# Three attention projection units moved in among the forms and first steps of the recurrence's first pair; query and key rotation released four copies sooner

## What is computed

```python
h = rms_norm(x, ln1_g[l]) * (1.0 + scale1) + shift1
z = jnp.einsum('bsd,de->bse', h, w_in[l])
y_a = rwkv7_time_mix(z_rwkv, ...)
y_b = moba_attention(z_att, q_norm_g[l], k_norm_g[l])
merged = g_a * (y_a @ w_br_rwkv) + g_b * (y_b @ w_br_moba)
x = x + gate1 * (merged @ w_out)
x = x + gate2 * hierarchical_moe(h2, ...)
```

## Time and profile before

| what | us |
|---|---|
| median of 3 runs | 1046.7 (1045.08 to 1047.42) |
| the profiled execution's own time | 1044.92 |
| its span in the trace | 1043.0 |
| PE busy in the span | 996.4 (96%) |
| DVE, ACT, POOL busy | 526.4, 319.5, 130.0 |

### The profile page before, as it was taken

How to read it: one execution, slowest core, us unless ns; L and a number is a source line. 1 busy time by engine, 2 the same in 40 slices (tenths; PEclk the granted TensorE clock), 3 DMA queues, 4 the chain that set the end, 5 groups by cost and what they waited for, 6 DMA issues and landing times.

```text
span 1043.0 us, 17857 instructions
## 1 busy us (share of the span) xinstructions
PE 996.4 (96%) x7746; PEld 633.3 (61%) x7746; DVE 526.4 (50%) x809; ACT 319.5 (31%) x587; POOL 130.0 (12%) x152
## 2 busy tenths in 40 slices
PE   8999999998888899999999999999999999999998
PEld 6777899978775588788787333444344434344343
DVE  4668852146538875676566433433344333342354
ACT  4467743154546731232423211111111111111110
POOL 0000000376974400000001000000000000000000
PEclk9999999999989999999999999999999999999999
DMA  9622021000003078464779999999999999999993
GB/s 384 246 115 98 24 82 44 11 5 4 4 21 145 8 238 298 131 212 176 283 305 397 333 417 428 426 426 427 427 427 425 427 426 426 426 427 419 414 415 133
DMA packets 42975, 273.24 MB, mean 262 GB/s; under 512 B 8032, under 2 KB 8176, under 8 KB 28688
## 3 DMA queue, kind: packets, MB, share of 16 engines
q1 hardware_dynamic: 39488, 264.42, 63.0%
q0 software_dynamic: 2400, 4.28, 1.2%
q10 hardware_dynamic: 1008, 3.38, 0.9%
HBM read 272.06 MB, written 4.19 MB: 265 GB/s over the span
## 4 chain that ended last, share of the span: by engine, by line
PE 80%; DMA 8%; DVE 7%; ACT 3%; issue 1%; SPq 0%; DVEq 0%; POOLq 0%; ACTq 0%
PE banks L1777 30%; PE banks L2336 19%; PE banks L2350 9%; DMA w_tok<-in_w 4%; DMA w_qkv<-in_w 3%; PE banks L2374 2%; PE banks L2375 2%; PE banks L2342 2%; PE banks L2322 1%; ACT xT L977 1%; PE banks L1940 1%; PE banks L1955 1%; PE banks L1957 1%; DVE ring L1397 1%; PE banks L1915 1%
## 5 line engine op out<-in xcount | busy, mean ns | idle before, releaser
L1656 DVE TENSOR_TENSOR hid<-banks,silu_a 64x512 f32<-64x512 f32 x32 | 22.2, 693 | 199.1 <-ACT silu_a L982 199.1
L2350 PE MATMUL banks<-w_ring,hidT 128*64 128x512 f32 x512 | 116.8, 598 | 1.1 <-ACT hidT L986 1.1
L1643 DVE SCALAR_TENSOR_TENSOR mod<-banks,row_weight,mod 64x512 f32<-64x512 f32 x64 | 47.9, 748 | 70.3 <-PE banks L2350 69.3
L982 ACT ACTIVATE silu_a<-banks 64x512 f32<-64x512 f32 x32 | 18.9, 591 | 207.7 <-PE banks L2337 207.7
L2337 PE MATMUL banks<-w_tok,xT 128*64 128x512 f32 x176 | 79.6, 606 | 0.0
L2336 PE MATMUL banks<-w_tok,xT 128*64 128x512 f32 x176 | 78.3, 596 | 0.3 <-DMA w_ring<-in_w 0.3
L2337 PE MATMUL banks<-w_ring,xT 128*64 128x512 f32 x176 | 78.3, 596 | 0.0
L1650 DVE TENSOR_TENSOR x<-x,banks 128x1024 f32<-128x1024 f32 x60 | 71.8, 1219 | 12.6 <-PE banks L2375 12.2
L2336 PE MATMUL banks<-w_ring,xT 128*64 128x512 f32 x160 | 72.4, 606 | 3.3 <-DMA w_qkv<-in_w 3.3
L2350 PEld LDWEIGHTS banks<-w_ring,hidT 128*64 128x64 f32 x512 | 34.3, 136 | 67.0 <-issue 65.8
L1777 PE MATMUL banks<-x_r,ring_r 128*128 128x512 f32 x192 | 74.8, 390 | 0.0
(11 more groups left out here) (387 smaller groups left out, 2180.0 us busy)
## 6 DMA issues: line engine op xcount, KB each, us to landing
w_ring<-in_w SPq DMA_DIRECT2D x42, 2048.0 KB, 25.2
w_tok<-in_w SPq DMA_DIRECT2D x16, 2048.0 KB, 26.0
ada_buf<-in_w_ada SPq DMA_DIRECT2D x64, 256.0 KB, 3.5
w_ab<-in_w SPq DMA_DIRECT2D x8, 2048.0 KB, 25.5
w_qkv<-in_w SPq DMA_DIRECT2D x7, 2048.0 KB, 29.3
w_tok<-in_w SPq DMA_DIRECT2D x24, 512.0 KB, 16.6
w_ring<-in_w SPq DMA_DIRECT2D x24, 512.0 KB, 17.3
w_ring<-in_w SPq DMA_DIRECT2D x10, 1024.0 KB, 15.5
```

What stands on the lines that cost most here:

```text
L1643: dve.scalar_tensor_tensor(dst[:, 512 * n:512 * n + 512], bank[5][SLOTS * n:SLOTS * n + SLOTS, :], weight_of(e), gate2[:, n, :], ALU.mult, ...
L1656: dve.tensor_tensor(hid[:, :], bank[3][SLOTS:P, :], silu_a[:, :], ALU.mult).then_inc(hid_v, 1)
L2350: mm = pe.matmul(bank[5][SLOTS * n:SLOTS * n + SLOTS, :], hidT[:, k, :], w2[:, k, 512 * n:512 * n + 512], start=(k == 0), stop=(k == 3))
```

## The change

Nothing is computed differently; instructions are moved on four engines, and the dummy matmuls of the recurrence are gone.

- PE: forms of groups 0 and 1 come behind unit 20, units 21, 22 and 23 stand between the first steps of pair_a, and the forms of groups 2 and 3 stand between its levels, behind waits on att_out of 11 and 12. Pair_b starts one level of pair_a later than before, so it is two levels behind. Its last steps (m5, wu, gh) run on into the next half. In half 1 the chains and outputs of half 0's last two chunks are spread over more of pair_a's steps.
- ACT and DVE: the same copies and masks in the order that this asks for; ACT takes copy 10 and copy 11 between the recurrence's copies, and the square root (and DVE's reciprocal) for the rotation comes right behind pair_b's r0 and first inverse.
- DVE at the end of half 1: both queries_added of pair_b stand ahead of next_state.
- POOL: the wait on att_out asks for 8 in place of 12.

The diff, cut in ACT's loop, whose rest mirrors the PE loop:

```diff
--- before.py
+++ after.py
@@ -744,8 +744,8 @@
             att_copy(7)
             cut_first("att", 5, 0)
             cut_first("att", 5, 1)
-            for g in range(8, 12):
-                att_copy(g)
+            att_copy(8)
+            att_copy(9)
 
             def end_keys(half, k):
                 sc, g = 2 * half + k // 2, k % 2
@@ -782,43 +782,53 @@
             for k in range(NG):
                 end_keys(0, k)
             act.activation(small[:, 57:58], one, ACT.Sqrt)
+            att_copy(10)
             for half in range(2):
                 solve_copy(half, "x", *pair_a)
                 if half:
+                    solve_copy(0, "h", *pair_b)
+                solve_copy(half, "r0", *pair_a)
+                if half == 0:
+                    att_copy(11)
+                solve_copy(half, "n1", *pair_a)
+                if half:
                     out_copy(0, 2)
-                solve_copy(half, "r0", *pair_a)
+                solve_copy(half, "r1", *pair_a)
                 if half:
                     out_copy(0, 3)
                     for k in pair_b:
                         end_keys(1, k)
-                solve_copy(half, "n1", *pair_a)
-                solve_copy(half, "r1", *pair_a)
+                solve_copy(half, "n2", *pair_a)
+                solve_copy(half, "r2", *pair_a)
                 solve_copy(half, "x", *pair_b)
                 solve_copy(half, "r0", *pair_b)
-                for n in range(2, 5):
+                if half == 0:
+                    act.wait_ge(ssq_qk, 1)
+                    act.activation(rms_qk, ssq, ACT.Sqrt).then_inc(sqrt_qk, 1)
+                for n in range(3, 5):
...
@@ -1015,7 +1025,7 @@
-            pool.wait_ge(att_out, 12)
+            pool.wait_ge(att_out, 8)
@@ -1277,7 +1287,6 @@
-            dve.wait_ge(att_mm, 12)
@@ -1342,37 +1351,47 @@
             for half in range(2):
                 first_inverse(half, *pair_a)
                 if half:
+                    state_factors(0, *pair_b)
+                    queries_added(0, 2)
+                level_masked(half, 1, *pair_a)
+                if half:
                     queries_added(0, 3)
                     next_state(0, 2)
+                else:
+                    masked_forms(0, 2)
+                level_masked(half, 2, *pair_a)
+                if half:
                     next_state(0, 3)
-                level_masked(half, 1, *pair_a)
-                for k in pair_b:
-                    masked_forms(half, k)
-                level_masked(half, 2, *pair_a)
+                    masked_forms(1, 2)
+                masked_forms(half, 3)
+                level_masked(half, 3, *pair_a)
                 first_inverse(half, *pair_b)
-                for n in range(1, 4):
-                    level_masked(half, n, *pair_b)
-                    level_masked(half, n + 2, *pair_a)
-                    if n < 3:
-                        chunk_decays(2 * half + n - 1)
-                level_masked(half, 4, *pair_b)
-                state_factors(half, *pair_a)
-                queries_added(half, 1 - half)
-                level_masked(half, 5, *pair_b)
-                queries_added(half, half)
                 if half == 0:
                     dve.wait_ge(sqrt_qk, 1)
                     dve.reciprocal(ssq, rms_qk).then_inc(rstd_qk, 1)
+                    dve.wait_ge(att_mm, 12)
+                for n in range(1, 3):
+                    level_masked(half, n, *pair_b)
+                    level_masked(half, n + 3, *pair_a)
+                    chunk_decays(2 * half + n - 1)
+                level_masked(half, 3, *pair_b)
+                state_factors(half, *pair_a)
+                level_masked(half, 4, *pair_b)
+                queries_added(half, 1 - half)
+                queries_added(half, half)
+                if half == 0:
                     next_state(0, 1)
+                    level_masked(0, 5, *pair_b)
                     masked_forms(1, 0)
                     masked_forms(1, 1)
                 else:
                     next_state(1, 0)
+                    level_masked(1, 5, *pair_b)
                     next_state(1, 1)
-                state_factors(half, *pair_b)
-                queries_added(half, 2)
+            state_factors(1, *pair_b)
+            queries_added(1, 2)
+            queries_added(1, 3)
             next_state(1, 2)
-            queries_added(1, 3)
 
             def norm_inverse(half):
                 c = slice(256 * half, 256 * half + 256)
@@ -1888,12 +1907,11 @@
-            for u in range(16, 6 * TT):
+            for u in range(16, 21):
                 att_unit(u)
 
-            pe.wait_ge(att_out, 12)
             pe.wait_ge(prep_done, CT)
-            pe.wait_ge(turn_a, TT * CT)
+
             def head_of(k, i):
 
                 h = 4 * (k % 2) + i
@@ -2012,66 +2030,76 @@
                 for _ in range(n):
                     pe.matmul(dst, ident, ident, start=True, stop=True)
 
-            for k in range(NG):
-                forms(0, k)
-                if k < NG - 1:
-                    between(bank[7][:, 0:P], 4)
+            forms(0, 0)
+            forms(0, 1)
+            att_unit(21)
             for half in range(2):
-                for k in pair_a:
-                    if half == 0:
-                        pe.wait_ge(solve_v[k], v_at(0, "tt"))
-                        between(bank[2 * k][:, 256:256 + P], 6)
-                    solve_step(half, "t0", k)
+                solve_step(half, "t0", 0)
+                if half == 0:
+                    att_unit(22)
+                    pe.wait_ge(turn_a, TT * CT)
+                solve_step(half, "t0", 1)
+                solve_step(half, "x", *pair_a)
+                if half:
+                    solve_step(0, "gh", *pair_b)
+                solve_step(half, "r0", *pair_a)
+                if half == 0:
+                    att_unit(23)
+                solve_step(half, "p1", *pair_a)
                 if half:
                     chain(0, 2)
-                solve_step(half, "x", *pair_a)
+                else:
+                    pe.wait_ge(att_out, 11)
+                    forms(0, 2)
+                solve_step(half, "n1", *pair_a)
                 if half:
                     outputs(0, 2)
-                solve_step(half, "r0", *pair_a)
+                else:
+                    pe.wait_ge(att_out, 12)
+                    forms(0, 3)
+                solve_step(half, "r1", *pair_a)
                 if half:
                     chain(0, 3)
-                solve_step(half, "p1", *pair_a)
+                solve_step(half, "p2", *pair_a)
                 if half:
                     outputs(0, 3)
                     forms(1, 2)
                     forms(1, 3)
-                solve_step(half, "n1", *pair_a)
-                solve_step(half, "r1", *pair_a)
+                solve_step(half, "n2", *pair_a)
+                solve_step(half, "r2", *pair_a)
                 solve_step(half, "t0", *pair_b)
-                solve_step(half, "p2", *pair_a)
+                solve_step(half, "p3", *pair_a)
                 solve_step(half, "x", *pair_b)
                 solve_step(half, "r0", *pair_b)
-                for n in range(2, 5):
+                for n in range(3, 5):
                     solve_step(half, f"n{n}", *pair_a)
-                    solve_step(half, f"p{n - 1}", *pair_b)
+                    solve_step(half, f"p{n - 2}", *pair_b)
                     solve_step(half, f"r{n}", *pair_a)
-                    solve_step(half, f"n{n - 1}", *pair_b)
+                    solve_step(half, f"n{n - 2}", *pair_b)
                     solve_step(half, f"p{n + 1}", *pair_a)
-                    solve_step(half, f"r{n - 1}", *pair_b)
+                    solve_step(half, f"r{n - 2}", *pair_b)
                 solve_step(half, "m5", *pair_a)
+                solve_step(half, "p3", *pair_b)
+                solve_step(half, "wu", *pair_a)
+                solve_step(half, "n3", *pair_b)
+                solve_step(half, "gh", *pair_a)
+                solve_step(half, "r3", *pair_b)
                 solve_step(half, "p4", *pair_b)
-                solve_step(half, "wu", *pair_a)
+                if half:
+                    chain(1, 0)
                 solve_step(half, "n4", *pair_b)
-                solve_step(half, "gh", *pair_a)
+                outputs(half, 0)
                 solve_step(half, "r4", *pair_b)
+                chain(half, 1)
+                outputs(half, 1)
                 solve_step(half, "p5", *pair_b)
                 if half == 0:
-                    outputs(0, 0)
-                    solve_step(0, "m5", *pair_b)
-                    chain(0, 1)
-                    outputs(0, 1)
                     forms(1, 0)
-                    solve_step(0, "wu", *pair_b)
+                solve_step(half, "m5", *pair_b)
+                if half == 0:
                     forms(1, 1)
-                    solve_step(0, "gh", *pair_b)
-                else:
```

(9 more changed lines are left out.)

16 lines of the change are left out of this document (8 added, 8 removed).

## The result

The changed kernel takes 1039.65 us (median of 5 runs, 1036.47 to 1040.1) against 1046.7 (5 runs, 1044.07 to 1048.81): a ratio of 0.9926 with a 95% interval of 0.9901 to 0.9951, 7.1 us less. The forecast was 8.8 less, 1037.9. Its profiled execution took 1040.1 us, with a span of 1038.3.

What follows compares the result with a forecast made beforehand. The recurrence was taken as bound by a ring of short dependent steps through PE's in-order queue: its work plus gaps. Gains 7.3 − 0.5 + 2.0 = 8.8 us took the 1046.7 median to 1037.9, range 1034.0 to 1042.2.

Steps and rivals of the forecast that it cites:

- Stretch one: Recurrence up to r0 of pair_b in half 0 (219.88 before): r0 at 212.6, a gain of 7.3 us.
- The second way of counting: Stretch to pair_b's r0, half 0: dummies 6.3, copy 11 wait 0.7, t0 waits 1.5, others 0.5, level costs 1.7; claimed 7.3.
- Stretch two: From there to r0 of pair_b in half 1 (268.15 before): net cost 0.5 us, between 0 and 2.
- Stretch three: From r0 of pair_b in half 1 to the recurrence's end: net gain 2.0 us, between 0.5 and 3.5.
- the clock term: PE's falls to 1.2 GHz in the recurrence: same cost as before, 2.8 us less or more as ends.
- tail: End of half 1, queries ahead of next_state: PE's 1.4 us wait and part of the chain's go, 1.9 us gained.
- The rotation: POOL starts 23.6 us earlier, rotation from near 215 to 269, ACT without a wait; its earlier end costed at nothing.
- Downstream one to one: Merge and experts: a recurrence that ends earlier moves their start, and the expert loads' start, by as much.
- Rival 1: Two-level lag's PE gaps lower the clock twice more, stretch two at upper bound: gain 4.5, 1042.2 us; chance 0.09.
- Rival 2: Norms come late, ACT waits with the recurrence's copies queued behind: 7.9 us slower, 1054.6 us; chance 0.04.
- Rival 3: Merge or experts wait for something the earlier stage does not move: 1046.7 ± 1 us; chance 0.03.
- Rival 4: Units among the forms delay pair_a, stretch one gives only the dummies: gain 6.1, 1040.6 us; chance 0.09.

Runs made afterwards that it cites:

- the changed kernel's second: The changed kernel itself, unedited, timed and profiled again beside other kernels on one chip: 1039.25 us (8 runs), ratio 0.993.
- the units alone: Kernel before with units 21 to 23 among the forms, no dummies, POOL's wait at 8, pair_b one level behind, old tail and square root: 1037.94 us.
- the two cures: Changed kernel with, ahead of chain(1, 0) in half 1, either six dummy matmuls (1031.61 us) or n4 of pair_b (1031.51 us); two separate kernels.
- the fillers: Changed kernel with six dummy matmuls on PE ahead of chain(1, 0) in half 1: 1031.61 us, ratio 0.9851.
- both cures: Changed kernel with n4 of pair_b, then six dummy matmuls behind the wait for ACT's gh copy, ahead of chain(1, 0) in half 1: 1032.32 us.
- n4 first with fillers at t0: Changed kernel with n4 of pair_b ahead of chain(1, 0) and six dummy matmuls between pair_b's two t0 in half 1: 1034.46 us.
- the held-back POOL: Changed kernel with POOL's wait on the projection copies put back from 8 to 12: 1060.92 us, ratio 1.0128.
- The fillers at t0: Six dummy matmuls between pair_b's two t0 in half 1, added to the changed kernel with n4 first (1034.46 us) or with chain(1, 0) dummies (1036.0 us).
- n4 first: Changed kernel with n4 of pair_b put ahead of chain(1, 0) on PE in half 1: 1031.51 us, ratio 0.9859.

## Why the prediction was right, and where it was off

*Stretch one* was forecast to gain 7.3 us and gained 7.4: r0 of pair_b at 212.48 for 212.6, t0 of group 0 at 194.84 for 194.9 (units 21 and 22 took 3.06 each where I had 2.91), t0 of group 1 at 198.52 for 198.3. The walk of PE's queue was right almost piece by piece: from the first form of half 0 to the r0 it has 22.7 us, and the trace 22.61. The end of 0.1 us is partly luck, since the forms start at 189.9 in some profiles and 1.1 to 1.3 us later in others, the changed kernel's second among them (191.07, r0 at 213.68, a gain of 6.2). The second way of counting, which was to confirm the 7.3, was added up wrongly: 6.3 + 0.7 + 1.5 − 0.5 − 1.7 is 6.3, so it did not confirm it. That dummies on the chain are removable work is shown by the run without them, and that units in their place are worth more is shown by the units alone (8.1 us by medians). The 1.7 us in it for the extra level is right: with pair_b one level behind, in the kernel of the units alone, r0 comes 20.84 us behind the first form, 1.8 less.

*Stretch two* was to cost 0.5, between 0 and 2, and gained 0.25 in the first profile and 2.7 in the second (45.54 us for 48.27). So this term had the wrong sign. The wait for pair_b's masks stayed, 1.66 us ahead of 257.03, as forecast; a fall of the clock of some 3.4 us came behind it in the first profile and none in the second, where the wait was 1.45.

*Stretch three* was to gain 2.0, between 0.5 and 3.5, and lost 2.8, 3.0 in the second profile. This is the step that failed, together with the clock term, "the same cost as before", with ends of 2.8 either way. The *tail* in it was undersized: 3.2 us measured for 1.9. The wait at chain(1, 0) came with 1.71 us, near the 1.6 I gave to the new gaps in sum. What failed is the price of a gap. I priced it at its own length plus falls like those of the earlier trace rows, 3.4 and 6.9 us long. The fall that came with it lasted 17.5 us in each of two profiles, and the two cures show its price: 5.4 and 5.1 us of stretch three (40.97 against 35.55 and 35.87), and none of it is the wait: with the fillers the chain step comes 18.5 us behind r0 (277.67 for 259.20), in the changed kernel's second profile 17.5 (276.73 for 259.22). PE's gaps did not grow in sum: it idles 4.6 us of this stretch, and 5.7 before; its busy time grew, at 1.2 GHz. With the clock up behind the chain step the stretch gains 2.3 to 2.6 on the 38.16 of before, inside my 0.5 to 3.5. With both cures the turned queries start 11.5 us sooner than before (294.80 for 306.31): 10.1 up to the r0 of pair_b in half 1 (258.09 for 268.15, with no fall near 257) and 1.4 behind it (with the late fall of some 7 us). The ratio of that kernel says 15 to 16 us in all; 2.2 more are in the length behind the recurrence (734.5 for 736.7), and the rest no run takes apart.

*The rotation* was right in every point: norms at 175.68 for 175.9, first rotation at 214.48 for 215, end near 269.7 for 269, no wait of ACT. The masks beside the norms took 0.43, 0.77 and 0.43 us: two keep the short time, one does not. The Trainium skill's GPSIMD Engine Reference, section Specifications, has VectorE instructions with two SBUF inputs contend with GpSimd; the 0.77 would fit it, but the 0.43 of 206.41 lies beside the same norm instruction of POOL, so the trace doesn't show the cause. It moved nothing: this mask ends at 194.8, and its reader, t0 of group 1, starts at 198.52.

*Downstream one to one* was right: from the turned queries to the end of the span it was 736.7 before and 736.8 after. In other profiles that length varies from 734.5 (the changed kernel's second) to 738.3 (n4 first with fillers at t0), with falls of the clock of about 3.5 us at changing places in the merge and experts. In the longest the end of a fall that began in the recurrence is part of it. That is a scatter of nearly 4 us, so a single profile of each kernel supports no smaller claim about a total.

*The total* was closer than its parts. From the kernel before to the changed kernel's first profile it is 7.4 + 0.25 − 2.8 − 0.1 = 4.7 us, to the second 6.2 + 2.7 − 3.0 + 2.2 = 8.1, where 7.3 − 0.5 + 2.0 + 0 was forecast. That the medians came out at 7.1 for 8.8 is in part luck: the third stretch lost 5 us against its forecast, and stretch two and the length behind the recurrence gave some of it back in the second profile.

*The rivals.* Rival 1, more half clock, came true in its kind, and the first profile pair's 4.7 is near its 4.5: that took in two falls like the old ones and the upper bound of stretch two; there was one long fall, about 5 us, and stretch two cost nothing. It was rated 0.09, which was too little: the earlier trace rows showed that a fall could last twice as long as another, and I took the two as the full scale of what can happen. Rival 2 did not occur, and its mechanism is real (21 us by the held-back POOL). Rival 3, hidden anyway, is excluded by the downstream length. Rival 4 is excluded by r0 at 212.48.

*Still open.* Why the falls at chain(1, 0) last 10.5 to 17.5 us while those near 257 last about 3.5, and what decides in one execution whether one comes: a wait of 1.45 us near 257 had a fall behind it in the kernel with fillers and none in the changed kernel's second profile. With the stretch ahead of the chain step filled on both sides the one profile has no fall there and no run of six is above 1033.91; n4 first with fillers at t0 shows that a short wait alone does not keep the fall away. The fillers at t0 were expected to help and did not.

## What to carry to other kernels

Dummy matmuls that stand on the chain of waits are a gap with a clock on it: with real, independent work there the kernel gained their whole length; with nothing in their place the next step came 4.3 us sooner for 6.3 us of dummies, and a third was left by the medians (2.1 us), in a kernel with more time at 1.2 GHz. When a reordering takes work of PE from one place, look at where PE becomes thin next, and price that by the work that runs behind it at 1.2 GHz, not by the wait alone. Six fillers in a wait of 1.7 us were worth some 8 us here by the medians, as much as the whole change, and 5 of these are shown to be the clock's. And where a wait is moved ahead of a queue of copies, work out the latest time at which its producer may end; here the earlier start of POOL was what kept 21 us away.

## What the runs showed that I had not expected

PE at 1.2 GHz while it is recorded busy for 16.91 of 17.50 us: the clock did not come back with the work, as the shorter falls of the earlier trace rows had let me assume, and stayed down for the same 17.5 us in the second profile. With fillers or n4 first the same matmuls behind the chain step ran at 2.4 GHz up to the turned queries, in one profile of each. The Trainium skill's TensorE: Matmul & The Clock Gate, section What's actually happening, has activity release the throttle; by it I had expected the clock back sooner, and here the rows differ.

The same kernel gives runs that lie up to 11 us apart (1029.09 to 1039.91 with n4 first), and with six fillers more the spread was 2.7 in six runs. Where a kernel has such a spread, the median of five or six runs tells in part how many of them fell into the upper part, so a difference under 3 us wants both kernels on one chip and more runs.

And a mask instruction of DVE (128 by 256) took between 0.42 and 1.30 us in one execution, the long ones while POOL rotated, as in the kernel before.
